# The solve of the mixing loop: triangular masks applied to N ahead of time, z copied out by ScalarE, adds on half of the columns, state update as a matmul and a ScalarE copy, and the chain begun in slot 0

## What is computed

```python
def step(state, inp):
    r_t, w_t, k_t, v_t, a_t, b_t = inp
    sa = jnp.einsum('bhvk,bhk->bhv', state, a_t)
    state = state * w_t[:, :, None, :] + sa[..., None] * b_t[:, :, None, :] + v_t[..., None] * k_t[:, :, None, :]
    return state, jnp.einsum('bhvk,bhk->bhv', state, r_t)
```

## Time and profile before

| | us |
|---|---|
| median of 3 runs | 3304.57 (3302.2 to 3304.61) |
| the profiled execution, its time | 3300.46 |
| the profiled execution, its span from first to last instruction | 3298.7 |
| TensorE busy | 2941.7 (89% of the span) |
| VectorE busy | 1682.8 (51%) |
| GpSimd busy | 1216.4 (37%) |
| ScalarE busy | 993.2 (30%) |
| mean granted TensorE clock | 0.95 |

### The profile page before, as it was taken

How to read it: one execution, slowest core, us unless ns; L and a number is a source line. 1 busy time by engine, 2 the same in 40 slices (tenths; PEclk the granted TensorE clock), 3 DMA queues, 4 the chain that set the end, 5 groups by cost and what they waited for, 6 DMA issues and landing times. The chain is left out here.

```text
span 3298.7 us, 61271 instructions
## 1 busy us (share of the span) xinstructions
PE 2941.7 (89%) x26974; PEld 2437.3 (74%) x26974; DVE 1682.8 (51%) x1907; ACT 993.2 (30%) x1542; POOL 1216.4 (37%) x603
## 2 busy tenths in 40 slices
PE   3899999996899999999999986797976799999995
PEld 2688888884688877788877765786755588887884
DVE  6654444444176666667666763113222744453445
ACT  2433333222233333333333421212221333333221
POOL 1444444442354433454443430222131344444441
PEclk7999999997999999999999997898988899999997
DMA  3222224433221111322111100611002122234441
GB/s 140 82 94 80 80 103 166 144 121 134 60 66 54 52 46 45 98 63 60 52 46 46 47 24 12 222 59 32 19 26 89 64 80 77 77 102 166 144 144 67
DMA packets 247429, 270.71 MB, mean 82 GB/s; under 512 B 13184, under 2 KB 204800, under 8 KB 245120
## 3 DMA queue, kind: packets, MB, share of 16 engines
q1 hardware_dynamic: 247168, 266.84, 24.5%
HBM read 218.57 MB, written 48.23 MB: 81 GB/s over the span
## 5 line engine op out<-in xcount | busy, mean ns | idle before, releaser
L460 POOL TENSOR_TENSOR w_low<-ffn_work,w_high 128x1024 fp32r<-128x1024 f32 x182 | 445.4, 2448 | 667.4 <-ACT w_high L533 394.2
L500 PE MATMUL bank<-h_high,w_high 128*128 128x512 f32 x1232 | 484.9, 394 | 57.2 <-DVE h_low L644 35.9
L500 PE MATMUL bank<-h_high,w_low 128*128 128x512 f32 x1232 | 483.4, 392 | 0.0
L500 PE MATMUL bank<-h_low,w_high 128*128 128x512 f32 x1232 | 483.4, 392 | 0.0
L691 DVE TENSOR_TENSOR h_low<-ffn_work,h_high 128x512 fp32r<-128x512 f32 x88 | 204.3, 2321 | 250.6 <-ACT h_high L548 250.6
L1076 POOL TENSOR_TENSOR mix_panel_low<-arena,mix_panel_high 128x1024 fp32r<-128x1024 f32 x96 | 240.6, 2506 | 233.5 <-ACT mix_panel_high L1426 233.4
L1164 PE MATMUL bank<-mix_h_high,mix_panel_high 128*128 128x512 f32 x768 | 312.3, 407 | 13.8 <-POOL mix_panel_low L1076 13.6
L500 PEld LDWEIGHTS bank<-h_high,w_high 128*128 128x128 f32 x1232 | 234.2, 190 | 109.6 <-issue 57.5
L1164 PE MATMUL bank<-mix_h_high,mix_panel_low 128*128 128x512 f32 x768 | 300.2, 391 | 0.0
L1164 PE MATMUL bank<-mix_h_low,mix_panel_high 128*128 128x512 f32 x768 | 300.1, 391 | 0.0
L517 PE MATMUL bank<-h_high,w_high 128*128 128x512 f32 x704 | 274.8, 390 | 4.5 <-DVE h_low L691 4.5
(11 more groups left out here) (261 smaller groups left out, 5667.0 us busy)
## 6 DMA issues: line engine op xcount, KB each, us to landing
arena<-w_in SPq DMA_DIRECT2D x96, 512.0 KB, 3.7
ffn_work<-w_down SPq DMA_DIRECT2D x88, 512.0 KB, 3.6
a_spill<-ffn_work SPq DMA_DIRECT2D x88, 256.0 KB, 2.2
ffn_work<-a_spill SPq DMA_DIRECT2D x88, 256.0 KB, 2.6
ffn_work<-w_gate SPq DMA_DIRECT2D x12, 1024.0 KB, 5.5
ffn_work<-w_up SPq DMA_DIRECT2D x12, 1024.0 KB, 8.1
arena<-x_spill SPq DMA_DIRECT2D x3, 4096.0 KB, 13.9
arena<-w_gate SPq DMA_DIRECT2D x10, 1024.0 KB, 5.4
```

The costliest lines, as they stand in the source:

```text
L460: nc.gpsimd.tensor_tensor(slot(w[1], q), src, slot(w[0], q).bitcast(F32), ALU.subtract).then_inc(s_low, 1)
L500: last = mm(bank[:, bk, :], w[wp][:, q % RING, kt, e], h[hp][:, k, kt], start=fresh and kt + wp + hp == 0, stop=kt == KT // 2 - 1 and wp = ...
```

## The change

- The mask of a level is no longer applied to z but to N, before the product: N is copied to SBUF unmasked by ScalarE (`n_raw`, in a buffer that is free then), and GpSimd makes the masked copy for levels 1 to 4, alternating between two buffers. VectorE masks N for level 0.
- z is therefore only copied from PSUM, by ScalarE (`z_stored`).
- In each level only every other block of columns of `xt` and of `x` changes, so VectorE adds only those: half of the elements.
- The state update loses VectorE: TensorE accumulates a third pair, the old state times a diagonal matrix of decays that is in SBUF already, and ScalarE copies the sum to the new state. The copy of the decays (`pend`) on GpSimd is dropped.
- The chain begins in slot 0 and ends in slot 23. Slots 24 to 27 have no chain step.

```diff
@@ gpsimd, prepare and solve @@
-                            G.tensor_copy(pend[i % 2].unsqueeze(2), ends).then_inc(S("ends_ready"), 1)
...
+                        pool.wait_ge(S("n_copied"), i + 1)
+                        for n in range(1, len(LEVELS)):
+                            if n > 1:
+                                pool.wait_ge(S("z_ready"), 10 * i + 2 * n - 2)
+                            G.tensor_tensor(n_st[n % 2][:], n_raw, over_chunks(c(f"join{LEVELS[n]}")),
+                                            ALU.mult).then_inc(S("n_masked"), 1)
@@ tensor, score_slot, level_slot, chain_step and the loop @@
                             elif s == 6:
                                 seen("n_stored")
+                                seen("n_copied")
...
+                                    seen("n_masked", 4, n)
...
                                 if part in (None, 1):
+                                    heads(bank[:, C, 2 * CH:3 * CH], old[:, n, 2, :], state[:, pb, n % 2, :],
+                                          start=False, stop=False)
...
-                            step = divmod(s - FIRST_CHAIN, 3) if back and s >= FIRST_CHAIN else None
+                            step = divmod(s, 3) if back and s < CHAIN else None
@@ scalar, solve @@
                             A(flat(x_st), bank[:, F3, :], ACT.Copy).then_inc(S("x_copied"), 1)
+                            seen("n_stored")
+                            A(flat(n_raw), bank[:, F0, :], ACT.Copy).then_inc(S("n_copied"), 1)
...
+                                else:
+                                    seen_back("state_sum_ready", n)
+                                    A(state[:, pb, (n + 1) % 2, :], bank[:, C, 2 * CH:3 * CH],
+                                      ACT.Copy).then_inc(S("state_ready"), 1)
+                            if live and s >= SCORES and quarter(s)[1] < 2:
+                                n, q = quarter(s)
+                                act.wait_ge(S("z_ready"), 10 * i + 2 * n + 1 + q)
+                                A(z_st[:, 4 * q:4 * q + 4], one(ZB[q])[:, 0:4], ACT.Copy).then_inc(S("z_stored"), 1)
@@ vector, solve @@
-                                V.tensor_tensor(part(z_st, q), one(ZB[q])[:, 0:4], over_chunks(c(f"join{LEVELS[n]}T"), 4),
-                                                ALU.mult).then_inc(S("z_stored"), 1)
...
+                            def columns(t, odd):
+                                return t.rearrange("p c (b two m) -> p c b two m", two=2, m=LEVELS[n])[:, :, :, odd]
...
+                            V.tensor_tensor(xt_q, columns(one(TB[q])[:, 0:4], 1), xt_q, ALU.add).then_inc(
+                                S("xt_added"), 1)
...
-                                    V.scalar_tensor_tensor(out=state[:, pb, (n + 1) % 2, :], in0=state[:, pb, n % 2, :],
-                                                           scalar=pend[b % 2][:, n:n + 1],
-                                                           in1=bank[:, C, 2 * CH:3 * CH], op0=ALU.mult,
-                                                           op1=ALU.add).then_inc(S("state_ready"), 1)
```

More of the change, by code:

```diff
@@ L41 @@
 SBUF_WORDS = 53200
-BASE_WORDS = 10180
+BASE_WORDS = 10116
 D = 1024
@@ L83, in constants @@
     for m in LEVELS:
-        parts[f"join{m}T"] = joins(m, j, i)
+        parts[f"join{m}"] = joins(m, i, j)
     where, at = {}, 0
@@ L957, in mixer @@
             mx, es, den = a2(NC), a2(NC), a2(NC)
-            pend = [a2(NC) for _ in range(2)]
             root_in, root, minus_half = a2(4, 2), a2(4, 2), a2(4, 2)
@@ L971, in mixer @@
             work = flat(prob)
-            n_st, z_st, x_st = by_chunk(work[:, 0:HALF]), by_chunk(work[:, HALF:T]), by_chunk(flat(prob_t)[:, 0:HALF])
+            x_st, z_st = by_chunk(flat(prob_t)[:, 0:HALF]), by_chunk(work[:, HALF:T])
+            n_st, n_raw = [by_chunk(work[:, 0:HALF]), by_chunk(flat(prob_t)[:, HALF:T])], by_chunk(t2)
             pex, pinv = ld, cum
@@ L1331, in level_slot @@
                                 else:
+                                    seen("n_masked", 4, n)
                                     seen("xt_added", 10, 2 * n - 1 + q)
                                 for m, at in enumerate(chunks):
-                                    last = to_other(one(ZB[q])[:, m, :], n_st[:, at, :], xt_new[:, at, :])
+                                    last = to_other(one(ZB[q])[:, m, :], n_st[n % 2][:, at, :], xt_new[:, at, :])
                                     if m == 3:
@@ L1528, in solve @@
                                 A(flat(k_tok[i % 2]), bank[:, F1, :], ACT.Copy).then_inc(S("k_tok_stored"), 1)
-                            if back and s >= FIRST_CHAIN:
-                                n, k = divmod(s - FIRST_CHAIN, 3)
+                            if back and s < CHAIN:
+                                n, k = divmod(s, 3)
                                 if k == 0:
@@ L1732, in solve @@
-                        for s in range(SLOTS):
-                            if live:
-                                if s == 0:
-                                    seen("n_ready")
-                                    V.tensor_tensor(n_st[:], one(F0), over_chunks(c("col_before_row")),
-                                                    ALU.mult).then_inc(S("n_stored"), 1)
-                                elif s in (1, 2):
-                                    store_base(s - 1)
-                                elif s in (4, 5):
-                                    store_before(s - 4)
-                                elif s >= SCORES:
-                                    level_slot(*quarter(s))
-                            if back and s >= FIRST_CHAIN:
-                                n, k = divmod(s - FIRST_CHAIN, 3)
-                                if k == 2:
-                                    seen_back("state_sum_ready", NC, n + 1)
-                                    seen_back("state_ready", NC, n)
-                                    V.scalar_tensor_tensor(out=state[:, pb, (n + 1) % 2, :], in0=state[:, pb, n % 2, :],
-                                                           scalar=pend[b % 2][:, n:n + 1],
-                                                           in1=bank[:, C, 2 * CH:3 * CH], op0=ALU.mult,
-                                                           op1=ALU.add).then_inc(S("state_ready"), 1)
@@ new lines, in level_slot @@
+                        def level_slot(n, q):
+                            def columns(t, odd):
+                                return t.rearrange("p c (b two m) -> p c b two m", two=2, m=LEVELS[n])[:, :, :, odd]
+                            seen("xt_grown", 10, 2 * n + 1 + q)
+                            if n > 0:
+                                seen("xt_added", 10, 2 * n - 1 + q)
+                            else:
+                                seen("xt0_ready", 2, q + 1)
+                            xt_q, x_q = columns(part(xt_new, q), 1), columns(part(x_st, q), 0)
+                            V.tensor_tensor(xt_q, columns(one(TB[q])[:, 0:4], 1), xt_q, ALU.add).then_inc(
+                                S("xt_added"), 1)
+                            if n < 4:
+                                seen("x_grown", 8, 2 * n + 1 + q)
+                                if n > 0:
+                                    seen("x_added", 8, 2 * n - 1 + q)
+                                V.tensor_tensor(x_q, columns(one(XB[q])[:, 0:4], 0), x_q, ALU.add).then_inc(
+                                    S("x_added"), 1)
@@ new lines, in solve @@
+                        if live:
+                            seen("n_ready")
+                            V.tensor_tensor(n_st[0][:], one(F0), over_chunks(c("join2")), ALU.mult).then_inc(
+                                S("n_stored"), 1)
+                            for q in range(2):
+                                store_base(q)
+                            for q in range(2):
+                                store_before(q)
+                            for n in range(len(LEVELS)):
+                                for q in range(2):
+                                    level_slot(n, q)
```

28 lines of the change are left out of this document (4 added, 24 removed).

## The result

The changed kernel takes 3339.61 us (median of 4, 3333.43 to 3342.13), the kernel before on the same chip 3304.59 (3302.2 to 3308.23): a ratio of 1.01, with a 95% interval of 1.0084 to 1.0116. I had forecast 3288 us. It is slower, by about 35 us.

What follows compares the result with a forecast made beforehand. The prediction took the chain, delayed by VectorE's queue at the state update, to pace the solve. Its terms gave -1.08 us a pass, -16.2 for fifteen, then -1.5 and +1.4: 3304.57 - 16.3 = 3288 us, range 3279 to 3300.

Steps and rivals of the forecast that it cites:

- Terms 1 to 5: Solve with a chain: slots without chain -1.93, fuller score slots +1.15, late ScalarE +0.74, k copy +0.38, last steps +0.23 us.
- terms 2 to 4: Early solve: more chain in score slots +1.15, ScalarE starting late +0.74, k copy ahead of sa's in slot 7 +0.38 us.
- term 3: Solve start: ScalarE, busy with earlier work and unmasked N, copies p1 late and TensorE waits, +0.74 us a pass.
- Term 6: State update on ScalarE: VectorE's queue goes, less the third pair, 0.33 us for each of five updates, -1.65 a pass.
- term 2: Score slots: eight chain steps of 21 pairs instead of four of ten, issue-bound, 10 x 0.115 = +1.15 us a pass.
- Pass 0 (-1.5): Pass without a chain: VectorE's six operations set 2.53 us a level, falling near 2.2 without masks, -1.5 us in all.
- The last chain (+1.4): Chain alone at the end, at clock 0.50: a pair costs twice 0.115, the copy saves 0.05, +1.4 us over eight.
- What I put at nothing: Three edits priced at zero: GpSimd's masks, half-width adds with a slot of slack, and `pend`'s copy in the prepare part.
- the masks did not slow VectorE: Rival that GpSimd's masks slow VectorE's work: 0.8 us a pass, 3317 us, 2 in 100; the forecast assumed no slowing.
- The clock: Rival: new idling in the solve lowers TensorE's clock; four more slow passes eat the gain, 3305 us, 5 in 100.
- ScalarE becomes the queue: Rival: z copies hold up the chain's copies on ScalarE, passes 1.1 us longer, about 3322 us, 8 in 100.

Runs made afterwards that it cites:

- stream: Kernel before with 1600 small matmuls over four quadrants, then 1600 over two, put ahead of the loop without waits: 3480.72 us, one run.
- masks alone: Changed kernel with the state update back on VectorE and the chain from slot 4, leaving masks, z copies and half-width adds: 3307.42 us, ratio 1.0001.
- two padded kernels: Changed kernel with 105 already met waits a pass (2560 TensorE instructions): 3349.41 us; the same with half a fetch more ahead of the loop: 3340.58 us.
- first padded kernel: Changed kernel with 105 already met waits a pass among the projections, making 2560 TensorE instructions: 3349.41 us.
- half columns: Changed kernel with growth matmuls moving only the columns that the half-width adds use, same number of instructions: 3339.4 us, ratio 1.009.
- double copy: Changed kernel with ScalarE copying each new state twice, first into a spare tile: 3339.8 us, ratio 1.0093.
- Merging: Products of b and k sharing a stationary tile merged, in kernel before, changed kernel and masks alone: 3325.91, 3360.31 and 3325.32 us.

## Why the prediction was wrong

- **Terms 1 to 5 (where the chain lies): about right.** Together +0.57 us a pass, or +8.5. The changed kernel less its variant with the chain from slot 4 is 3339.6 - 3330.05 = 9.6 us, or 15 by the ratios. The starts of the state copies bear out terms 2 to 4: 3.17 us after the first mask of N, then 3.73 and 3.83 apart in every undisturbed pass, and TensorE waited for p1 at the start of solve 9 as term 3 has it, 0.54 us where I had 0.74. With the update left on VectorE the same shift costs 27 us.
- **Term 6 (the update on ScalarE, -1.65 a pass): the step that failed.** I took "the 0.34 to 0.44 us of queue go" for time off the path, five times a pass. The queue did go: single intervals of 2.32 to 2.60 us between state copies stand where 2.52 to 2.93 stood, as forecast. But alone, with its third pair, the move costs 12.6 us by its ratio. The pair costs 1.0 to 1.2 us a pass, not the 5 x 0.115 I put in term 6 with two more in term 2 (0.8 in all), and the queue's end brings some 0.2 a pass instead of 2.2: the time was taken by TensorE's stops for instructions, 28.8 us in passes 1 to 13 where 4.6 stood.
- **The premise under it.** I wrote "TensorE never waits in these slots now (they are issue-bound)" and priced issue at 0.115 us a pair as if that pace could last. For four quadrants it can't, as the stream shows: 46 us of matmuls took 89. I also read the longest waits ("<-DVE L1749") as the bound. They were the cover of another one behind: with the masks alone 25.7 us of waits became 26.2 of "issue".
- **The sum as the runs have it,** by their ratios: +12.6 us for the update on TensorE and ScalarE, +6 for the masks on top of it, +15 for the chain from slot 0, together the 33 of the ratio 1.01. I had -25, nothing and +8.5 (and -0.1 outside).
- **Pass 0 (-1.5): wrong**, 60.77 us where it took 60.64. I took six VectorE operations for its pace, but TensorE was busy for 19.22 of the 19.59 us of solve 0, with 670 records, one in 29 ns. The masks left a queue that TensorE hardly waited for, and nothing came of it, as in the masks-only kernel (60.98).
- **The last chain (+1.4): about right.** State copies 3.09 apart, updates 2.94 before, 0.15 in each where I had 0.18.
- **What I put at nothing held.** The adds took 0.29 us with GpSimd's mask beside them (1605.26 and 1604.77), so the masks did not slow VectorE. The Trainium skill, "SBUF — State Buffer", "Who interferes with whom", says that a VectorE instruction with at most one input in SBUF, outside its 2-port modes, does not contend with GpSimd, and the trace agrees. The clock was 1.00 in every solve but solve 6, before and after, and fell there to 0.89 (0.95 before), but that pass grew by 2.3 us, no more than the others.
- **The rivals.** None named this one. "ScalarE becomes the queue" gave a time nearer the truth, 3322, by a mechanism that isn't there: no wait in the view ends with a z copy.

What is shown: supply limits a stream of such matmuls (stream); in the solve every "issue" time stands at the same point of a block of 256 instructions, and instructions put ahead move them (the two padded kernels); each lengthens its pass by its own length (first padded kernel); and in the changed kernel neither the columns nor most of 14 us of chain latency have a price (half columns, double copy). Merging lost its meaning to new waits. Not every microsecond of the loss is supply: the third pair keeps TensorE busy longer, and the early chain adds waits for ScalarE's copies. Open is what sets the length of a single stop. So is why the masks on top of the moved update cost 6 to 9 us (3320.76 to 3330.05), though alone they cost nothing; by the table it went into stops for instructions, 28.8 to 41.2 us.

## What to carry to other kernels

Where a stage runs many small matmuls over the quadrants of the array, count TensorE's instructions (two a matmul record) against its length before taking a wait off another engine: here 930 records in 27 us were already one in 29 ns, and the supply gave one in 27. A wait that ends last in the profile may cover another limit; a cheap probe is a doubled copy, which costs little or nothing where the chain is not the bound. Idle time that no engine ends is worth numbering: if it always falls at the same remainder of 256 instructions, it is the fetch. An operation that is moved to TensorE is not cheap because its columns are few.

## What the runs showed of the hardware, unexpected

- Four quadrants of 64 x 64 fp32 matmuls: 14.4 ns a record between gaps, 27.8 ns over the whole (89.0 us for 3200), a stop, most often of 1.36 us, once in 3.5 us with each 16 KB packet of instructions. Two quadrants: 29.4 ns, hardly a stop (0.2 us in all).
- In twenty traces each "issue" time of TensorE in these stretches, 769 in all, stands at the same point of a block of 256 instructions, and ends 2.2 to 3.0 us after a fetch began. Waits that stand by themselves count as instructions: each is 0.05 us long in the trace, and 1575 of them brought seven more fetches (222, of 215).
- Small matmuls between large ones cost 0.62 us a group of 4 to 20 records, some 0.35 of it for the change from one kind to the other.
- Two copies of 64 columns on ScalarE start 0.12 us apart, though each takes 0.22.
- Half a fetch of met waits ahead of the loop made the padded kernel 9 us faster.
